# Projection products shared out by VectorE's work, and a new order of parts, stores and copies in stick-breaking attention

## What is computed

```python
proj = rmsnorm(x, a_norm) @ w_in                 # q, k, v, gate: 4 x 1024 columns
z = (q @ k.T) / 8                                # per head, s < t only
w[t, s] = sigmoid(z[t, s]) * prod(1 - sigmoid(z[t, j]) for s < j < t)
o = (w @ v) * silu(gate)
out = rmsnorm(x + o @ w_out, final_norm)
```

## Time and profile before

| | us |
|---|---|
| median of the runs | 1628.62 |
| the profiled execution, its own time | 1635.98 |
| its span | 1634.2 |
| TensorE busy | 1573.5 (96%) |
| VectorE busy | 1282.4 (78%) |
| ScalarE busy | 883.9 (54%) |
| GpSimd busy | 414.0 (25%) |

### The profile page before, as it was taken

One profiled execution on the slowest core, in us unless ns is written; L12 is line 12 of the kernel. 1 busy time (PEld: TensorE's weight loads), 2 busy tenths in 40 slices (PEclk: granted clock), 3 DMA queues, 4 the chain that ended last, 5 costly groups with the idle time before them and its releaser, 6 DMA issues. The chain is left out here.

```text
span 1634.2 us, 46030 instructions
## 1 busy us (share of the span) xinstructions
PE 1573.5 (96%) x19314; PEld 1459.2 (89%) x19314; DVE 1282.4 (78%) x1525; ACT 883.9 (54%) x1558; POOL 414.0 (25%) x520
## 2 busy tenths in 40 slices
PE   9999989999999999999999999999999998999998
PEld 7888889899999999998999899999999998868887
DVE  4535338888888888897888898889889897967873
ACT  6635336566655666665655566656655665842221
POOL 0022033224323243323332433324422340000000
PEclk9999989999999999999999999999999999999999
DMA  9968643434334252434343343524253436779621
GB/s 306 274 180 272 183 142 109 124 111 124 124 105 122 88 156 76 140 94 129 105 121 115 111 118 102 152 73 140 81 157 87 123 102 204 249 248 318 203 103 65
DMA packets 205933, 238.57 MB, mean 146 GB/s; under 512 B 54560, under 2 KB 162080, under 8 KB 205728
## 3 DMA queue, kind: packets, MB, share of 16 engines
q1 hardware_dynamic: 113344, 160.30, 32.0%
q10 hardware_dynamic: 92384, 75.33, 15.2%
HBM read 155.78 MB, written 79.76 MB: 144 GB/s over the span
## 5 line engine op out<-in xcount | busy, mean ns | idle before, releaser
L957 PE MATMUL o_ps<-r_turned_hi,dv_head 64*128 64x512 f32 (+3 forms) x1280 | 481.4, 380 | 21.6 <-ACT o_stage L1190 19.7
L1400 DVE TENSOR_TENSOR_SCAN u<-u,u 128x512 f32<-128x512 f32 x384 | 485.5, 1304 | 0.0
L1179 ACT ACTIVATE u<-z_ps 128x512 f32<-128x512 f32 (+3 forms) x640 | 330.9, 533 | 265.1 <-PE z_ps L880 177.0
L923 PE MATMUL group_ps<-hT_hi,w_hi 64*128 64x256 f32 x1888 | 453.6, 281 | 2.9 <-DVE made L1384 2.0
L957 PE MATMUL o_ps<-r_turned_lo,dv_head 64*128 64x512 f32 (+3 forms) x1280 | 454.1, 365 | 0.0
L923 PE MATMUL group_ps<-hT_hi,w_lo 64*128 64x256 f32 x1888 | 448.8, 280 | 0.0
L923 PE MATMUL group_ps<-hT_lo,w_hi 64*128 64x256 f32 x1888 | 447.6, 279 | 0.0
L1404 DVE TENSOR_TENSOR r_turned_lo<-turn_ps,r_turned_hi 128x1024 fp32r<-128x1024 f32 (+1 forms) x320 | 337.5, 1055 | 130.6 <-ACT r_turned_hi L1184 129.8
L1184 ACT ACTIVATE r_turned_hi<-turn_ps 128x1024 fp32r<-128x1024 f32 (+1 forms) x320 | 287.5, 899 | 172.6 <-PE turn_ps L902 149.6
L923 PEld LDWEIGHTS group_ps<-hT_hi,w_hi 64*128 64x128 f32 x1888 | 318.5, 186 | 8.1 <-DVE made L1384 2.8
L923 PEld LDWEIGHTS group_ps<-hT_lo,w_hi 64*128 64x128 f32 x1888 | 314.4, 186 | 2.1
(11 more groups left out here) (180 smaller groups left out, 3253.2 us busy)
## 6 DMA issues: line engine op xcount, KB each, us to landing
qk_hi_cols<-made ACTq DMA_DIRECT2D x128, 128.0 KB, 2.4
qk_lo_cols<-made ACTq DMA_DIRECT2D x128, 128.0 KB, 2.5
k_hi_twice<-qk_hi_cols SPq DMA_DIRECT2D x128, 128.0 KB, 3.2
k_lo_twice<-qk_lo_cols SPq DMA_DIRECT2D x128, 128.0 KB, 3.6
x_T<-in_xT SPq DMA_DIRECT2D x29, 512.0 KB, 6.5
w_raw<-in_w_qkg SPq DMA_DIRECT2D x24, 512.0 KB, 4.0
x_rows<-in_x SPq DMA_DIRECT2D x16, 512.0 KB, 4.8
v_rows<-v_stage ACTq DMA_DIRECT2D x32, 256.0 KB
```

The source lines that it names most:

```text
L923: last = nc.tensor.matmul(bank_of(g)[:, 0:GW], a[t % 2][rows, k, :], b[rows, c // 2, k, cols], start=(n == 0 and not low), stop=(n == QPM ...
L957: last = nc.tensor.matmul(o_ps[:, 0:w], dv_head[rows, j * CB + sigma_block(m), :], turned_part[p % 2][rows, here], start=first, stop=(end ...
L1179: nc.scalar.activation(u_t[(m // CB) % RU][r][:, 0:w], score_bank(m), ACT.Sigmoid, scale=-Z_SCALE).then_inc(s_u, 1)
L1400: nc.vector.tensor_tensor_scan(u, u, other, start, ALU.mult, op).then_inc(s_r, 1)
```

## The change

It has five parts. First, `limits()` no longer releases 12 or 15 items: it works out for each half slot how long VectorE has work there (5.8 units for a column of a scan, 2.3 for a column of `lo`), takes off what TensorE has to do besides, smooths over three half slots, adds a constant so that the sum comes out, and caps a half slot at 16 items. Worked out, the shares by place are, for a middle head:

| place | 0 | 1 | 2 | 3 | 4 | 5 | 6 | 7 | 8 | 9 |
|---|---|---|---|---|---|---|---|---|---|---|
| before | 12 | 12 | 15 | 15 | 15 | 15 | 15 | 15 | 12 | 12 |
| after | 15 | 16 | 16 | 16 | 16 | 16 | 12 | 11 | 15 | 16 |

| place | 10 | 11 | 12 | 13 | 14 | 15 | 16 | 17 | 18 | 19 |
|---|---|---|---|---|---|---|---|---|---|---|
| before | 15 | 15 | 15 | 15 | 12 | 12 | 15 | 15 | 12 | 12 |
| after | 16 | 15 | 12 | 11 | 15 | 13 | 13 | 8 | 10 | 12 |

The stream ends in half slot 312 and not 311, and the last head takes 186 items and not 162. Second, a finished group is treated ahead of `hi` and `lo` only if its bank is wanted in the first half of this half slot's share (`needed_soon`, 30 of the 178 groups); for the others `made_high` and its store come behind `hi`, and `made_low` behind `lo`. Third, `store_low` moves behind both sigmoids. Fourth, `empty` moves between the two sigmoids. Fifth, lower-row items are issued within the loop only if they are at least 26 items behind the upper ones (the limit of the stream per product), the rest follows at the half slot's end, and the output blocks use the four bank pairs in turn from block 0 on. The later end of the stream also moves `WO_FROM`, the pieces of the last stage (by 2 to 4 steps), and `LOAD_W` by up to 2 steps.

```diff
-QUOTA = {True: 12, False: 15}
+STREAM_HALVES = 2 * (NU - 4)
+MOST = 16
+SCAN_COLUMN, LOW_COLUMN = 5.8, 2.3
+
+def spare_columns(h):
+    s, p = h // 2, h
+    low = blocks_of_pair(p) * P
+    scans = [CH - score_cols(m) for m in range(PAIR * h + LEAD_SCORES - PAIR, PAIR * h + LEAD_SCORES) if m < NS]
+    scored = [CH - score_cols(m) for m in range(PAIR * h + LEAD_SCORES, PAIR * h + LEAD_SCORES + PAIR) if m < NS]
+    weighed = 2 * blocks_of_pair(max(p - 1, 0)) * P
+    return SCAN_COLUMN * sum(scans) + LOW_COLUMN * low - low - weighed - 1.5 * sum(scored)
 
 def limits():
-    upto = [0]
+    each = [spare_columns(h) / (GW + 10) for h in range(STREAM_HALVES)]
+    spare = [sum(each[max(h - 1, 0):h + 2]) / len(each[max(h - 1, 0):h + 2]) for h in range(STREAM_HALVES)]
+    more = (STREAM + BEHIND - sum(spare)) / STREAM_HALVES
+    upto, total = [0], 0.0
     for h in range(2 * NU):
-        _, c, j, _ = STEPS[CB * (h // 2)]
-        upto.append(min(upto[-1] + QUOTA[c == j], STREAM + BEHIND))
+        total += spare[h] + more if h < STREAM_HALVES else 0
+        upto.append(max(upto[-1], min(round(total), STREAM + BEHIND, upto[-1] + MOST)))
     return upto
+
+def needed_soon(g, h):
+    again = (g + 3 - FIRST) * QPM - UPTO[h]
+    return again < (UPTO[h + 1] - UPTO[h]) // 2
...
         def y_banks(n):
-            return y_ps[max(n - 1, 0) % len(y_ps)]
+            return y_ps[n % len(y_ps)]
...
                         group_half(0)
-                        group_half(1)
+                        if made_so_far[1] + QPM + 2 <= made_so_far[0]:
+                            group_half(1)
...
                     for _ in range(min(abs(spare) // GW, left(h, idle))):
-                        group_half(idle)
+                        if not idle or made_so_far[0] == STREAM or made_so_far[1] + QPM + 2 <= made_so_far[0]:
+                            group_half(idle)
...
-                        if m == 0 and n == 1:
-                            pe.wait_ge(s_res, f + 1)
-                        if m == 0 and n == len(y_ps):
+                        if m == 0 and n == len(y_ps) - 1:
                             pe.wait_ge(s_ost, H * NC)
-                        if m == 0 and n >= len(y_ps) + 1:
+                        if m == 0 and n >= len(y_ps):
                             pe.wait_ge(s_res, 2 * (n - len(y_ps)) + f + 1)
...
-                        for g in finished(h - 1):
+                        soon = [g for g in finished(h - 1) if needed_soon(g, h)]
+                        for g in soon:
                             made_high(g)
                             store_high(g)
                         if inside(s):
                             hi(h)
                         for g in finished(h - 1):
-                            store_low(g)
+                            if g not in soon:
+                                made_high(g)
+                                store_high(g)
                         if inside(s + LEAD):
                             stick(first + LEAD_SCORES)
+                        if ended is not None and part == 0:
+                            empty(ended)
+                        if inside(s + LEAD):
                             stick(first + LEAD_SCORES + 1)
+                        for g in finished(h - 1):
+                            store_low(g)
...
-                        if ended is not None and part == 0:
-                            empty(ended)
...
-                        for g in finished(h - 1):
+                        soon = [g for g in finished(h - 1) if needed_soon(g, h)]
+                        for g in soon:
                             made_low(g)
                         if inside(s):
                             lo(h)
+                        for g in finished(h - 1):
+                            if g not in soon:
+                                made_low(g)
```

More of the change, by code:

```diff
@@ L155, with score_cols, sigma_block, turn_width @@
 BEHIND = 30
-QUOTA = {True: 12, False: 15}
-STREAM = (NG - FIRST) * QPM
+def score_cols(m):
+    _, c, j, r = STEPS[m]
+    return r * P if j == c else 0
+def sigma_block(m):
+    _, c, j, r = STEPS[m]
+    return CB - 1 - r if j == c else r
+def turn_width(m):
+    _, c, j, _ = STEPS[m]
+    return (sigma_block(m) + 1) * P if j == c else CH
+def blocks_of_pair(p):
+    return (turn_width(PAIR * p) + turn_width(PAIR * p + 1)) // P
+STREAM = (NG - FIRST) * QPM
+STREAM_HALVES = 2 * (NU - 4)
[8 more added lines that the diff above has]
+    return SCAN_COLUMN * sum(scans) + LOW_COLUMN * low - low - weighed - 1.5 * sum(scored)
 def limits():
-    upto = [0]
+    each = [spare_columns(h) / (GW + 10) for h in range(STREAM_HALVES)]
+    spare = [sum(each[max(h - 1, 0):h + 2]) / len(each[max(h - 1, 0):h + 2]) for h in range(STREAM_HALVES)]
+    more = (STREAM + BEHIND - sum(spare)) / STREAM_HALVES
+    upto, total = [0], 0.0
     for h in range(2 * NU):
-        _, c, j, _ = STEPS[CB * (h // 2)]
-        upto.append(min(upto[-1] + QUOTA[c == j], STREAM + BEHIND))
+        total += spare[h] + more if h < STREAM_HALVES else 0
+        upto.append(max(upto[-1], min(round(total), STREAM + BEHIND, upto[-1] + MOST)))
     return upto
@@ L213 @@
 LAST_SLOT = LAST_PIECE_STEP // CB
[L216 to L228, removed]
 def chunk_end(u):
@@ L239, in blocks_before @@
     return turn_width(m - 1) // P if m % PAIR else 0
-def blocks_of_pair(p):
-    return (turn_width(PAIR * p) + turn_width(PAIR * p + 1)) // P
 def inside(u):
```

## The result

The changed kernel takes 1647.12 us (median of 7 runs), the kernel before 1629.0 beside it: ratio 1.0093 [1.0068, 1.0117] (the brackets are a 95% interval), slower by 15 us; the medians themselves are 18 us apart. One of the seven runs took 2493.54 us at a granted clock of 0.555 and is not in the ratio. 1617 was said, so the time moved the other way; 1644 was the third rival.

The account below looks back on a forecast made before the run. TensorE, busy 96%, was taken to bind. Terms -14 (copy), -10 (shares), -3 (made_high), 0, +12 (made_low), +3 (tile), 0 sum to -12 from the 1628.62 us median: 1617, range 1603 to 1625 (0.45).

Parts of the forecast that it names:

- the third rival: Slower: made_low behind lo holds the first item of the group three later; +15, so 1644 us; slower case's chance 0.22.
- The copy: At chunk ends, copying the output bank between the sigmoids shortens TensorE's wait for o_ps: -14 us, ends 0 and -19.7.
- `store_low`: Behind the sigmoids, it frees ScalarE's waits, but TensorE hardly ever waits for a sigmoid: 0 us, ends -5 and +5.
- `made_low` behind `lo`: Later bank release makes TensorE wait at a later group's first item: 46 places, 20.6 us; taken as +12, ends 0 and +31.
- `made_high` behind `hi`: Groups' high parts no longer delay hi, which counts where TensorE waits on lo: -3 us, ends 0 and -9.
- The shares: New items per half slot cover TensorE's waits for lo, less some new waits: -10 us, ends -21.9 and +8.
- The end of the stream and the last stage: Pieces 2 to 4 steps later still come in time; extra last-head items come from earlier heads: 0 us, ends -2 and +2.
- The weight tile: Steps 262 and 542: a late-scaled tile makes ScalarE wait, now at another place too: +3 us, ends 0 and +6.
- point of decision: The bank wait behind lo makes the kernel slower from 27 us on, a mean 0.33 us at 81 places.
- two signs that were to show me wrong: Group products wait under 5 or over 25 us; or waits fall as said and the middle stage is no shorter.
- The fourth rival: Another engine binds, so shares give 0 and the copy's 14 meets the bank's 12; no chance apart from the no-change case's 0.13.
- The rule of the Trainium skill on the order of matmuls: Matmuls start and end in program order; by it TensorE needs 3.67 us a half slot, so at most 34 us could be won.

Follow-up runs that it names:

- x8: Kernel before with only the copy moved between the sigmoids and store_low behind both; old shares, group parts ahead of hi and lo: ratio 0.9909.
- x1: Changed kernel with needed_soon always true, so every finished group's high and low parts stand ahead of hi and lo again: 0.9983, 1626.23 us.
- x3: Kernel before with only the copy of the output bank moved between the two sigmoids: 0.99, 1613.15 us.
- x5: Kernel before with only store_low moved behind both sigmoids: ratio 0.999.
- x2: Changed kernel with the old released items (12 and 15); orders of parts, store and copy as changed: ratio 1.0051.
- x7: Changed kernel with the lower rows 26 items behind the upper ones and not 30: ratio 1.0044.
- x12: Changed kernel with ScalarE's made_high and its store ahead of hi for every group; VectorE's made_low stays behind lo where it was: ratio 1.0196.
- x11: Changed kernel, but a group's parts stay ahead of hi and lo whenever its bank is wanted anywhere in this half slot's share: ratio 0.9966.
- x10: x9 with parts behind hi and lo only for groups whose bank is not wanted in the same half slot: 0.9843, 1602.07 us.
- x9: x1 with the new shares only in heads 0 to 14, at 276 items a head, and the last head's old 162 items: ratio 0.9865.
- z3: x9 with the last stage's pieces placed as in the changed kernel, four ScalarE works in half slot 309, no more products: ratio 0.9872.
- z1: x1 with the last stage's pieces spread, so ScalarE has two of these works in half slot 309 and not four: ratio 0.9962.
- y1: x1 with the weight tile of step 542 rounded 13 steps behind its load and not 9: ratio 0.9998.
- y2: x9 with the last head's load of the gating piece, and the pieces hanging on it, four steps later: ratio 0.9895.

## Why the prediction was wrong, by its steps

The terms measured in the order x8, x1, after add up: -15 (copy and store) + 12 (the shares) + 18 (the parts) = +15, where -12 was said.

**The copy**: right. -14 was said, -16 measured (x3); the wait under 8 us came (7.8 in x3, 6.9 in after).

**`store_low`**: right at 0 (x5).

**`made_low` behind `lo`**: the failed step that weighs most, and it failed in the price of the wait, not in the wait. Counted were 46 waits and 20.6 us, the trace has 47 and 23.1; a bank free 3.45 us behind the turns was said, and it is 3.42 in the half slot shown. I took +12 of it, since "Where VectorE is the one that binds (places 2, 10) they cost nothing". They cost 18 us with the new shares (after less x1, 17.8 us less of these waits) and 23 with the old (x2 less x8): the whole of the waits reached the end. VectorE gave no cover: its own wait for `hi` is 121.4 us in x1 and 146.0 in after, so it grew with TensorE's. x7, where these waits are gone and 0.0061 is not, says that they need not be all that such an order costs.

**`made_high` behind `hi`**: -3 was said. Given that `made_low` stands behind `lo`, it is worth 0.0103, 17 us (x12), for it brings `hi`, `lo` and so `made_low` forward. In itself it was not tried; all harmless groups behind, both parts, gain 0.0017 and 0.0022 (x11 less x1, x10 less x9), the size that was said and too small to tell.

**The shares**: -10 was said, and with 276 items a head and the old last head they gain 7 us (x9 less x8). As they were made they cost 12 us (x1 less x8). The wait of the turns for `lo` fell to 15.3 us, not to 8 to 14. Of the 19 us between x1 and x9 half lies in the next step and half in heads 1 to 14 (9.8 us by profile): that the gain would come with the shares as made failed too. The late weight tile is some 2 to 4 us of it (head 13), and the cause of the rest stays open.

**The end of the stream and the last stage**: 0 was said, with the argument that 24 items of the last head were taken from earlier ones. That step failed: from half slot 300 on x1 takes 92.51 us where x9 takes 82.80. Of these 9.7 us, 6.7 lie in half slots 310 to 312 (18.0 less 11.3), where the pile, the clock behind it and 13 of the 24 items fall; the pile with no more items makes 3.8 there (z3 less x9), the items with no pile 0.6 (z1 less x9). 1.0 lies in half slot 313, 1.6 in half slot 316, where the clock was 0.74 and 1.00, and 0.4 in the ten ahead. The text had the pieces "2 to 4 steps later" and asked only whether they came in time for the last stage, not what else stands in the half slot that they came to.

**The weight tile**: +3 was said. The wait came (2.9 us in the profile of after). Its price could not be told from nothing in the runs (y1); by the length of head 13 in the profiles it is 2.2 us.

**The rivals.** The third named the mechanism and its total (+15), with other terms: bank +31, shares -5 and tile +3 for 18, +12 and about 0. So that its total came true is in part luck. Its point of decision, 27 us for the bank, was not reached; the shares and the last head made up the rest. Of the two signs that were to show me wrong, the first did not come (the group products waited 23.1 us, under the 25), and the second came in part only: the middle stage was no shorter, but of the waits only the copy's fell as said. The fourth rival had the shares at 0, which is near what they gave in heads 1 to 14, and missed the last head. The rule of the Trainium skill on the order of matmuls ("TensorE: Matmul & The Clock Gate", section "The mechanism"), weighed in the prediction, bore neither on the sign nor on a term; no run here went below the 3.67 us a half slot that the count gives by it, the least is 3.69 (x10, 1033.77 us for half slots 20 to 299).

What stays open: why heads 1 to 14 gain with 276 items a head and not with 274 or 275; what the fifth part costs or gives by itself; what the low clock in half slots 311 to 312 costs by itself, since it came again in half slot 316 in several kernels (0.57 in after, 0.53 in z1, 0.60 in before, 1.00 in x9), and why there.

## What to carry to other kernels

Where one engine binds, take a wait of its own at the full price unless you can name, place by place, the engine that is later still; a mean idle time elsewhere is no cover. And lay two profiles side by side by stretch before you give a loss to a place: half of what the last head seemed to cost lay ahead of it. A part that frees a buffer may go behind other work only where the next use is beyond the half slot's own work, a condition that is worked out per buffer (x11: 81 of 148 groups made all the cost). And when the length of one stream moves what hangs on its end, list for every engine what now falls into the same place, as four small works ahead of `hi` did here.

## What the runs showed of the hardware

Behind a stand of TensorE in half slot 310 (2.9 us in after and x1, 2.4 in z3) the granted clock fell to 0.64 and 0.68 (after), 0.57 and 0.50 (x1), 0.61 and 0.62 (z3) for the next two half slots. 1.00 is 2.4 GHz and 0.50 is 1.2 GHz; a value between is a mean over the stretch. In z1, with waits of 0.9 us there, it stayed at 1.00. Not every stand is followed by it for so long: around the copy's wait in half slot 301 (4.5 us in after) the clock was 0.69 on the mean, and half slot 302 ran at 1.00 in 3.61 us. The Trainium skill says that the low clock is the default and activity releases it ("TensorE: Matmul & The Clock Gate", section "What's actually happening"); the falls behind these stands agree with that.

What the clock costs is seen in half slot 316, whose program is the same in x8 and x9: 4.84 us at 1.00 (x9) and 7.77 at 0.56 (x8). These 2.9 us are more than the whole of the 2.4 by which x9's last head is shorter than x8's.

The first head (half slots 0 to 19) took from 73.6 to 82.8 us in profiles of kernels that hardly differ there, so stretches were compared and not spans. It was long where the clock was low at its start: 73.7 us in y2 and 74.7 in x8 without that, 82.8 in before and 82.2 in x9 with 10 to 14 us at 0.50 from about 235 us on.
